# Expert rows kept in slot order: plain pair transfers in the loop, indirect scatters before it and indirect gathers after it

## The reference

```python
hx = _rms(x, norm_ffn[l]) * (1 + sc_fx) + sh_fx
x = x + g_fx * _moe(hx, router_w, router_b, exp_w1[l], exp_w3[l], exp_w2[l])

def _moe(h, ...):                      # 16 experts in 4 groups, 2 experts for each token
    aff = sigmoid(h @ router_w)
    ...                                # best group by its two best scores, then the two best in it
    wts = wts / sum(wts)               # gates, two for each token
    for e in range(N_EXPERTS):
        y = (silu(h @ w1[e]) * (h @ w3[e])) @ w2[e]
        out = out + gates[..., e:e+1] * y
```

## Time and profile before

| | us |
|---|---|
| median of 3 runs | 662.51 |
| span of the profiled execution | 715.4 |
| PE busy in it | 635.5 |
| DVE busy | 403.5 |
| ACT busy | 207.3 |
| POOL busy | 198.6 |

### The profile page before, as it was taken

One profiled execution on the slowest core, in us unless ns is written; L12 is line 12 of the kernel. 1 busy time (PEld: TensorE's weight loads), 2 busy tenths in 40 slices (PEclk: granted clock), 3 DMA queues, 4 the chain that ended last, 5 costly groups with the idle time before them and its releaser, 6 DMA issues.

```text
span 715.4 us, 15191 instructions
## 1 busy us (share of the span) xinstructions
PE 635.5 (89%) x5773; PEld 396.9 (55%) x5773; DVE 403.5 (56%) x950; ACT 207.3 (29%) x534; POOL 198.6 (28%) x244
## 2 busy tenths in 40 slices
PE   0899999999989989999996299999899998999994
PEld 0456544554444535555565257676676665676663
DVE  4814995577877767867744534444344344344342
ACT  5311201468884025554644000110101101101100
POOL 3054880000000010000002244444444544544541
PEclk9999999999999999999995589999999999999999
DMA  8987538333022749100089689999999758998200
GB/s 307 387 289 234 167 128 301 117 112 117 0 103 75 247 151 270 24 1 0 1 318 389 248 323 417 421 420 408 361 410 411 293 196 345 405 421 342 76 31 10
DMA packets 50003, 165.87 MB, mean 232 GB/s; under 512 B 5920, under 2 KB 22520, under 8 KB 39712
## 3 DMA queue, kind: packets, MB, share of 16 engines
q1 hardware_dynamic: 40560, 143.69, 52.7%
q0 software_dynamic: 9264, 21.43, 9.0%
q10 hardware_dynamic: 128, 0.04, 0.0%
HBM read 159.20 MB, written 9.98 MB: 236 GB/s over the span
## 4 chain that ended last, share of the span: by engine, by line
PE 68%; DVE 13%; issue 7%; another core or an unknown queue 5%; ACT 5%; DMA 1%; ACTq 0%; DVEq 0%; POOL 0%; POOLq 0%
PE bank L1716 21%; PE bank L1731 9%; PE bank L1520 9%; PE bank L1630 7%; PE bank L1446 6%; PE bank L1453 4%; PE bank L1607 2%; PE bank L1582 2%; PE bank L1593 2%; DVE acct L928 1%; PE bank L1665 1%; DVE pre L1323 1%; ACT hx L580 1%; ACT pre L649 1%
## 5 line engine op out<-in xcount | busy, mean ns | idle before, releaser
L1520 PE MATMUL bank<-ring,hx 128*128 128x512 f32 x256 | 114.4, 602 | 5.6 <-DVE mix L982 4.9
L1716 PE MATMUL bank<-pre 128*32 128x256 f32 x1248 | 91.4, 387 | 16.2 <-DVE pre L1332 6.4
L1716 PE MATMUL bank<-ring,pre 128*32 128x256 f32 x1152 | 82.0, 381 | 7.5 <-issue 4.1
L766 ACT ACTIVATE pre<-bank 128x128 f32<-128x128 f32 x44 | 12.2, 278 | 260.3 <-PE bank L1716 159.8
L1520 PEld LDWEIGHTS bank<-ring,hx 128*128 128x128 f32 x256 | 48.5, 193 | 64.1 <-issue 59.0
L1716 PEld LDWEIGHTS bank<-pre 128*32 128x32 f32 x1248 | 61.4, 111 | 40.1 <-issue 25.5
L1332 DVE TENSOR_TENSOR pre<-pre,ab 128x256 f32<-128x256 f32 x44 | 18.8, 427 | 102.1 <-PE bank L1716 56.4
L1716 PEld LDWEIGHTS bank<-ring,pre 128*32 128x32 f32 x1152 | 53.5, 110 | 31.6 <-issue 23.5
L1630 PE MATMUL bank<-ring,mix 128*128 128x512 f32 x128 | 60.7, 594 | 0.0
L1731 PE MATMUL bank<-pre 128*32 128x256 f32 x704 | 52.8, 380 | 1.7 <-DVE pre L1343 1.4
L1343 DVE STREAM_TRANSPOSE pre<-pre 128x128 f32<-128x128 f32 x44 | 18.8, 426 | 59.8 <-remote 40.5
(11 more groups left out here) (296 smaller groups left out, 1080.6 us busy)
## 6 DMA issues: line engine op xcount, KB each, us to landing
pre<-in_exp_w_dram SPq DMA_DIRECT2D x28, 1024.0 KB
ring<-in_exp_w_dram SPq DMA_DIRECT2D x24, 1024.0 KB
ring<-in_w_mod_dram SPq DMA_DIRECT2D x16, 1024.0 KB, 5.2
pre<-in_exp_w_dram SPq DMA_DIRECT2D x8, 2048.0 KB
ring<-in_exp_w_dram SPq DMA_DIRECT2D x6, 2048.0 KB
ring<-in_w_in_dram SPq DMA_DIRECT2D x5, 2048.0 KB, 14.3
ring<-in_w_mod_dram SPq DMA_DIRECT2D x4, 2048.0 KB, 18.1
mix<-in_exp_w_dram SPq DMA_DIRECT2D x6, 1024.0 KB
```

The lines of the kernel that those rows point to most:

```text
L1520: ins = te.matmul(B[bank][:, :], hxT[:, k, P * j:P * (j + 1)], slot[:, k, :], start=(k == 0), stop=(k == KD - 1))
L1716: ins = te.matmul(H_[R * q:R * (q + 1), 0:2 * P].rearrange("p (w n) -> p w n", w=2), hsT[:, R * k:R * (k + 1)], w[:, k % 4, :, P * q:P * ( ...
```

## The change

The rows of a token are no longer fetched by token, but put in slot order once. DVE computes one slot number for each token and choice (`slot_of`, 32 times the tile base plus the rank). After that POOL scatters each block of `xn` twice, once for each choice, into a table `slot_rows` of 1920 rows by 1024 columns in HBM: eight indirect DMAs of 128 rows of 4 KB. The table was filled before that, by 15 DMAs on SP's queue, each from a block of ones. The one-hot products and the tables of tokens and gates are gone.

In the loop, rows move for two tiles at a time and by plain DMAs on POOL's queue. One load and one store of a pair are four DMAs each, one for each quarter of the columns. The stored rows are expert outputs times `g_fx`, without gate and without the residual, and go back to their own slots. ACT's index copies and DVE's addition of old rows are gone.

At the end, POOL waits for all stores, then eight indirect gathers bring back both choices of each 128-token block. DVE multiplies with the gates and adds the residual, which was parked in HBM in `residual_rows` and is fetched back by SP as one 2 MiB DMA behind the weights. SP writes the output in four DMAs.

The order of SP's chunks changes too: chunk 8 waits for all eight scatters (`slots_out`), 9 for the parked residual, 10 for the plan.

```diff
+            sp.wait_ge(consts_ready, 1)
+            for n in range(MAXT * R // P):
+                sp.dma_start(slot_rows[P * n:P * (n + 1)].rearrange("p (k n) -> p k n", k=KD),
+                             ones[:].unsqueeze(1).to_broadcast([P, KD, P])).then_inc(slots_filled, 16)
             sp.wait_ge(lru_done, MW)
             fetch(0)
...
-            sp.wait_ge(xn_out, 8 * NT)
-            sp.wait_ge(xn_out1, 8 * NT)
+            sp.wait_ge(slots_out, 16 * 2 * NT)
             fetch(8)
             sp.wait_ge(h2_ps, 2 * NT)
-            sp.wait_ge(acc_in, 16 * NT)
-            sp.wait_ge(slots_turned, 1)
-            sp.wait_ge(xg_in[0], 16)
-            sp.wait_ge(xg_in[1], 16)
+            sp.wait_ge(res_out, 16 * NT)
             fetch(9)
+            sp.wait_ge(plan_in, 1)
             fetch(10)
...
-            sp.wait_ge(all_out, 1)
+            for j in range(NT):
+                sp.wait_ge(sums_added, 2 * (j + 1))
+                sp.dma_start(out_cols[QC * j:QC * (j + 1)], expert_sums[0][j]).then_inc(all_out, 16)
+            sp.wait_ge(all_out, 16 * NT)
...
+            pool.wait_ge(xn2_ready, NT)
             pool.wait_ge(slots_turned, 1)
+            pool.wait_ge(slots_filled, 16 * (MAXT * R // P))
+            for k in range(2):
+                for j in range(NT):
+                    g.indirect_dma_start(out=slot_rows, out_offset=bass.IndirectOffsetOnAxis(
+                        ap=slot_of[:, NT * k + j:NT * k + j + 1].bitcast(U32), axis=0), in_=xn[:, j, :], in_offset=None,
+                        bounds_check=MAXT * R - 1, oob_is_err=False).then_inc(slots_out, 16)
+            def load_rows(h, a):
+                if not isinstance(h, int) or h:
+                    pool.wait_ge(rows_taken, 4 * h + 2 * a - 2)
+                    pool.sem_inc(pool_step, 1)
+                src = slot_tiles(h, a)
+                for q in range(CB):
+                    g.dma_start(xg[a][R * q:R * (q + 1), :].rearrange("t (i n) -> t i n", i=2),
+                                  src[:, q]).then_inc(xg_in[a], 16)
+            def store_sums(h, a):
+                pool.wait_ge(y_ev, 4 * h + 2 * a + 3)
+                ...
+            pool.wait_ge(slots_out, 16 * 2 * NT)
+            load_rows(0, 0)
+            load_rows(0, 1)
...
+            with pool.Fori(1, last) as h:
+                load_rows(h + 1, 0)
+                store_sums(h - 1, 1)
+                load_rows(h + 1, 1)
+                store_sums(h, 0)
+            store_sums(last - 1, 1)
+            store_sums(last, 0)
+            store_sums(last, 1)
+            stored = pool.snap(64 * last + 64)
+            for a in range(2):
+                pool.wait_ge(y_out[a], stored)
+                pool.sem_inc(pool_step, 1)
+            for j in range(NT):
+                for k in range(2):
+                    g.indirect_dma_start(out=expert_sums[k][j], out_offset=None, in_=slot_rows,
+                                         in_offset=bass.IndirectOffsetOnAxis(
+                                             ap=slot_of[:, NT * k + j:NT * k + j + 1].bitcast(U32), axis=0),
+                                         bounds_check=MAXT * R - 1, oob_is_err=False).then_inc(back_in[j], 16)
...
-                v.scalar_tensor_tensor(out=ysb[i], in0=Y_[:, 0:QD], scalar=gate_tab[:, bass.ds(4 * h + i, 1)],
-                                       in1=gfx4, op0=ALU.mult, op1=ALU.mult).then_inc(y_scaled, 1)
-                dve.wait_ge(r_in[i], 16 * h + 16)
-                dve.wait_ge(y_scaled, 4 * h + i + 1)
-                v.tensor_tensor(ysb[i], ysb[i], rr[i], ALU.add).then_inc(y_ev, 1)
+                v.tensor_tensor(ysb[i // 2][:, QD * (i % 2):QD * (i % 2 + 1)], Y_[:, 0:QD], gfx4,
+                                ALU.mult).then_inc(y_ev, 1)
...
+            dve.wait_ge(res_back, 16)
+            for j in range(NT):
+                dve.wait_ge(back_in[j], 32)
+                for k, base in enumerate((residual_back, None)):
+                    if k:
+                        dve.wait_ge(sums_added, 2 * j + 1)
+                    v.scalar_tensor_tensor(out=expert_sums[0][j], in0=expert_sums[k][j], scalar=gatew[:, k, j:j + 1],
+                                           in1=expert_sums[0][j] if k else base[:, j, :], op0=ALU.mult,
+                                           op1=ALU.add).then_inc(sums_added, 1)
```

More of the change, by code:

```diff
@@ L46 @@
 ORDER = [EG * (i % NG) + i // NG for i in range(NE)]
-TRASH = T * CB
 ROUND = 1.5 * 2.0 ** 28
@@ L136, in build @@
         rt = pre[:, 12288:14336]
-        xg = [pre[:, 20480:20736], hx[:, 4608:4864], hx[:, 5504:5760], hx[:, 5760:6016]]
+        xg = [hx[:, 4096 + 2 * QD * a:4096 + 2 * QD * (a + 1)] for a in range(2)]
         xm = pre[:, 20736:20992]
@@ L143, in build @@
         eT = pre[:, 21504:21632]
-        ysb = [pre[:, 21632:21888], pre[:, 21888:22144], hx[:, 4864:5120], hx[:, 5120:5376]]
+        ysb = [gax[:, 2 * QD * a:2 * QD * (a + 1)] for a in range(2)]
         gfx4 = pre[:, 22144:22400]
@@ L207, in build @@
+        xg_in = [sem(f"rows_in{a}") for a in range(2)]
+        y_out = [sem(f"sums_out{a}") for a in range(2)]
+        back_in = [sem(f"sums_back{j}") for j in range(NT)]
         xsem = [sem(f"x_in{j}") for j in range(NT + NC)]
@@ L493, in scatter @@
-            def scatter(par):
-                g.indirect_dma_start(out=out_rows, out_offset=bass.IndirectOffsetOnAxis(
-                    ap=cur_s[par][:].bitcast(U32), axis=0), in_=ysb[par], in_offset=None, bounds_check=TRASH - 1,
-                    oob_is_err=False).then_inc(y_in[par], 16)
-            pool.wait_ge(xn_out, 8 * NT)
-            pool.wait_ge(xn_out1, 8 * NT)
-            pool.wait_ge(slots_turned, 1)
-            for n in range(4):
-                gather(slot_tok[:, n:n + 1], n)
+                g.dma_start(residual_rows[j], x2[:, j, :]).then_inc(res_out, 16)
@@ L557, in _ @@
-            for i in range(4):
-                landed = pool.snap(16 * last + 16)
-                pool.wait_ge(y_in[i], landed)
-                pool.sem_inc(pool_step, 1)
-            pool.sem_inc(all_out, 1)
+            load_rows(1, 0)
+            load_rows(1, 1)
+            store_sums(0, 0)
+            with pool.Fori(1, last) as h:
[4 more added lines that the diff above has]
+            store_sums(last - 1, 1)
@@ L1695, in _ @@
                       stop=True).then_inc(rank_ps, 1)
-            pe.wait_ge(oh_ready, 3)
-            for n in range(2 * NT):
-                for q in range(CB):
-                    ins = te.matmul(B[6][R * q:R * (q + 1), 0:2 * MAXT], oh_row[:, n, :], oh_val[:, n, :],
-                                    start=(n == 0), stop=(n == 2 * NT - 1))
-            ins.then_inc(oh_used, 1)
             def products(n, e, first):
```

245 lines of the change are left out of this document (46 added, 199 removed).

## The result

The changed kernel takes 713.99 us (median of 4 runs, 712.51 to 715.96), the kernel before 662.69 beside it (662.47 to 664.8). The ratio is 1.0776 (95%: 1.0747 to 1.0805): slower, as forecast, but 23 us above the predicted 691 and outside the range.

A forecast was written before the change was run, and what follows sets the result against it. The prediction took PE work as the bound, with one hole ahead of the expert loop. Hole +9.3, end +23.1, fill 0 and loop -3 on 662.5 gave 691.9, forecast 691 us; range 676 to 708 (0.8).

The forecast's parts named there:

- Ahead of the hole: Before the router's idle stretch of PE: the table's 7.9 MB fill on SP's queue costs 0, bounds 0 and +10.
- The hole: From ranks to first expert matmul: scatters and first loads replace one-hot work, +9.3 us, bounds 6.5 and 17.
- the landing beside the chunks: In the hole: first loads, sharing engines with 6 MB of weight chunks, land 3.5 us after their last issue.
- The loop: Expert tiles: PE's instructions stay the same, less row traffic gives -3 us in runs, bounds 0 and -14.
- the weights keep up: In the expert loop: DMA engines are full in first-half windows, but 33% free at 560 to 600 us.
- nothing is late: In the loop: POOL's row loads and stores have some three tiles (17 to 20 us) of lead.
- Rival 1: In the loop: weights bind in unprofiled runs, so the whole 14 us come back, 681 us; chance 0.14.
- Rival 3: In the loop: each of 22 pair transfers lands 1 to 2 us too late, 714 to 736 us; chance 0.08.
- The end: After the last DVE result: last stores, eight gathers, final sums and output write add 23.1 us, bounds 18 and 30.
- rival 5: Scatters and final gathers: indirect DMAs of 4 KB rows build descriptors slower; at twice the pitch 710 us; chance 0.08.
- Profile against runs: In the loop: most of the 52.9 us gap is PE's 70.3 us of "issue" waits; unprofiled tile 5.6 us.
- Rival 2: In the loop: PE's "issue" waits come from crowded DMA and indirect transfers and fall, 651 us; chance 0.04.

The follow-up runs named there:

- the quicker profile: The kernel before, unchanged, profiled once more: 663.16 us (0.9999), span 659.4.
- hold_chunks: Changed kernel with SP issuing weight chunk 8 (9 and 10 behind it) only when the first pair of tiles has landed: 710.03 us (0.9819).
- before_no_old: Kernel before without its gather of old output rows, 4.2 MB of DMA traffic less: 670.49 us (1.0134).
- no_loads: Changed kernel without the loads of expert rows from the third pair on, so later tiles use stale rows: 699.77 us (1.0557).
- spread_parts: Changed kernel with each load reading the same addresses but writing every fourth partition instead of 32 side by side: 695.03 us (0.964).
- block_one: Changed kernel with one load a pair over all partitions, from 256 KB side by side, columns not in the reference's order: 696.58 us (0.9691).
- before_third: Kernel before, unchanged, with a profile, on the chip of a set where it takes 721.1 us: 724.0 us from one run.
- the third set: A later set of runs on another chip, with the unchanged changed kernel at 714.47 us beside the kernel before at 721.1.
- after_pad: Changed kernel with 64 small matmuls, whose result nothing reads, at the start of PE's program: 715.54 us (0.9977).
- no_stores: Changed kernel without the stores of expert rows in the loop: 699.29 us (1.055).

## Why the prediction was wrong

Against the quicker profile of the kernel before the change costs 54.1 us of span (713.5 - 659.4); the prediction had 29.4.

- **Ahead of the hole**, predicted 0, measured +2.1: ranks are ready at 399.53 against 397.44. PE's clock drops 3.2 us earlier there (380.1 instead of 383.3). In the other profiles of either kernel the ranks are ready anywhere from 397 to 401, so this is scatter. The fill does no harm: the output projection's last matmul ends at 375.0 us in both.
- **The hole**, predicted +9.3, measured +14.3 (12.95 to 27.2), inside my bounds of 6.5 to 17. The scatters were right (pitch 1.27 instead of 1.33, landed 14.8 us after the ranks instead of 14.4). The term that was mis-sized is the landing beside the chunks: 3.5 us after its last issue by the share of bytes, and 8.3 in fact (425.1 less 416.8). `hold_chunks` shows that the chunks are the cause: 1.8 us without them.
- **The loop**, predicted -3, measured +14.9 (242.9 to 257.8, up to the last DVE result). This is the step that failed, 18 of the 25 us: the loop's term, with "the weights keep up", "nothing is late" and bounds of 0 and -14. It had two faults. I counted bytes wrongly: the kernel before skips the padding of its tiles and moves 12.6 MB of rows (not 17), the changed kernel moves all 1408 slots twice, 11.5 MB, so only 1 MB is saved and not 5.8. And I took 407 GB/s as given, where the form of the loads sets it: 382 instead of 419. So PE waits 10.8 us for weights instead of 0.9, and its clock is low for some 14 us after these waits. Rival 1 had the weights nearly bind the kernel before; they don't (0.9 us, and 0.7 us of loop for 4.2 MB in `before_no_old`), they bind the changed one. Rival 3 had the row transfers late; it is the weights that are. `no_loads`, `spread_parts` and `block_one` give the loop back (240.0, 238.3, 239.8), and none of the three runs that only moved the pieces in memory did.
- **The end**, predicted +23.1, measured +22.9 (6.1 to 29.0). That it fits so well is luck in part: the last gather comes 14.8 us after the last DVE result (predicted 15.4), but its landing takes 7.4 us instead of 3.9, and the last write with what follows 4.2 instead of 7.8, and the two errors cancel. The gathers' pitch of 1.30 holds for rows of 4 KB, so rival 5 falls.
- **Profile against runs.** I put the 52.9 us between them on 70.3 us of PE's "issue" pauses. That was a misreading of the earlier trace rows, whose 70.3 us count matmuls and weight loads, which overlap, one after the other; PE's matmuls have 12.7 of it. The quicker profile has fewer pauses in either count (17.7 and 4.4) and a loop 55 us shorter, 5.5 us a tile where I had estimated 5.6. So the place of the gap was right, and its size came out for the wrong reason. Most of the 55 us isn't in the idle time at all: PE's busy time falls from 635.5 to 594.6, since a pause shorter than a matmul's 0.38 us from start to end leaves PE counted as busy. And the cause isn't profiling, since a profile at 659.4 exists.
- **The baseline.** Unpriced was that the kernel before itself has two speeds. Rival 2 held that the change would take the pauses away. In the changed kernel they are few in both its profiles (21.1 and 27.3 us in the one-line view, 73.1 in `before_third`), also where the kernel before has them. Whether the indexed transfers made them, as rival 2 says, isn't shown. Where the kernel before is slower, the change about breaks even: 0.9893 (0.9861 to 0.9925) in the third set, and 0.9977 (0.9952 to 1.0001) for `after_pad` in the fourth. "Slower by 7.8%" belongs to the quicker speed.

## What to carry to other kernels

Where the DMA engines are full, the form of a small transfer counts as much as its bytes: loads that wrote 32 neighbouring partitions lowered the rate of the core by a tenth, and writing the same bytes four partitions apart was worth 19 us, more than leaving out the stores (15 us). The form on the memory side counts too, so measure each form: a load to all 128 partitions was slower still when its walk through memory was nested. Before counting saved bytes, look whether masked or skipped rows ever moved. Compare idle times only within one view. And when a profile's span and the runs differ by 8%, get a profile at the speed of the runs before pricing a loop.

## What the runs showed of the hardware

- Weights' packets of 8 KB have a median of 309 to 313 ns alone and beside indirect gathers and scatters or plain stores, and of 352 to 435 ns beside plain loads to 32 neighbouring partitions (`no_stores`); the core's rate is 372 to 384 GB/s with such loads in the loop, and 423 to 425 with the same loads four partitions apart.
- Indirect DMAs of 128 rows of 4 KB have the pitch of those of 1 KB (1.27 and 1.30 us) and land after 4.2 and 5.6 us (medians).
- Four plain DMAs of 64 KB, issued together with 6 MB of weights on another queue, were whole 8.3 us after the last issue, and 1.8 us without the weights.
- A plain DMA whose memory side takes two nested steps across its partitions, the outer one of four, lands after 11.5 to 14.8 us instead of 6.3, and the stores on the same queue with it. It comes with 16-byte packets, 96 for 128 KB and 24 for 32 KB, which fit four busy and twelve idle DMA engines.
- A kernel can run at 662 us in one set of runs and at 717 to 722 in four others on other chips, with pauses on TensorE at the change from tile to tile that follow neither its DMA load nor a shift of its code by 63 matmuls, while another kernel with the same matmuls in its loop stays at 714.
